# Results of a projection taken one group later beside attention, an output's remainder ahead of the next row maximum, and the products around them reordered, on one Trainium2 core

## The chip, the core and the metric

One core of a Trainium2 chip runs the whole program in one launch. Its engines run side by side, each through its own list of instructions, and wait for one another by semaphores: TensorE (PE; its weight loads are shown apart as PEld), VectorE (DVE), ScalarE (ACT), GpSimd (POOL), and SyncE (SP), which issues the weight transfers. The metric is the device time of one execution in microseconds (us).

## The reference

Two transformer networks follow each other, each of two layers, over 256 tokens of 1024 values; the first also carries 256 context tokens. First network: in each layer a gated feed-forward, a mixer (retention in layer 0, neighbourhood attention with 16 heads in layer 1), another feed-forward. Second network, cut to what matters here:

```
def second_block(x, positions, rel_bias, ...):
    for l in range(DEPTH):
        h = _rms_norm(x, norm_mix_pre[l])
        dq, dk, dv, mq, mk, mv, c_q, c_kv, k_pe, g = split(h @ w_in[l])
        oa = _diff_attention(dq, dk, dv, lam, rel_bias)      # 4 heads, two softmaxes each
        oa = _rms_norm(oa, diff_subln[l]) * (1.0 - lam_init)
        ob = _moba_attention(mq, mk, mv, rel_bias)           # 4 heads of 128
        q  = _rms_norm(c_q, mla_q_norm[l]) @ mla_w_uq[l]     # 8 heads, rope on 32 of 96
        kv = _rms_norm(c_kv, mla_kv_norm[l]) @ mla_w_ukv[l]
        oc = _dense_causal_attention(q, k, kv[v part], 1 / sqrt(96))
        br = stack(oa, ob, oc) @ w_branch[l]
        mixed = sum(sigmoid(g) * br) @ w_out[l]
        x = x + _rms_norm(mixed, norm_mix_post[l])
        h = _rms_norm(x, norm_mlp_pre[l])
        u = square(relu(h @ w_up[l]))
        x = x + _rms_norm(u @ w_down[l], norm_mlp_post[l])
    return x
```

Neighbourhood attention adds a bias per head and masks keys outside a window of 8 x 16 positions before the softmax. With 256 tokens MoBA has one block, so its attention is causal attention with a bias.

## The kernel before, in words

**One product.** Activations stay in SBUF, columns on partitions, tokens along a row. Every large product is float32 made of three fp32r products: high times high, high times low, low times high (`products`, matmul L1829). Weights come in blocks of 256 columns, 1024 deep, as two halves. SyncE loads them ahead into six raw slots; ScalarE copies a rounded high part (L808), VectorE subtracts it for the low part (L1215), each into one of three slots. A gemm is a list of groups, normally one block wide, two or four chunks of 128 columns or tokens each. TensorE writes the chunks in turn into four PSUM banks (gemm0 to gemm3); chunk n waits until chunk n − 4 is taken out. VectorE and ScalarE take it out as its kind says (`gemm` of each engine).

**The order** is written out by hand, once for each engine. `splits_upto` puts the splits of the next weight block between the chunks of the current one.

**Attention** is a generator of steps on each engine, a step for each head and half of 128 queries. TensorE issues scores (L1905; bias or mask L1906) into aux0 or aux1, turns the probabilities by a multiplication with a diagonal of inverse sums (L1922, aux2), and multiplies them with v (L1936, aux3). VectorE takes the row maximum (L1411, L1412), makes the diagonal (L1421, L1424; L1427 for the negated half of differential attention) and an output's low part (L1436); in neighbourhood attention it also adds the mask to a head's bias table (L1447). ScalarE makes exponentials (L974), copies turned probabilities out (L955) and the output's high part (L963).

**`alongside`** interleaves these steps with groups of other gemms: beside the four neighbourhood groups of four heads (`nat0` to `nat3`) the q, k, v of the next four heads, 9 groups in all; beside differential attention MoBA's k and v; beside latent attention (MLA) branch0, gate1, branch1 and gate2. `lag` says how many steps later than TensorE's list the other two engines' lists have the group: 1 beside the narrow attentions (differential, MoBA, MLA), 0 beside neighbourhood attention.

**The second network's layer** in order: the latents (mla_c), differential q, k, v, the two latent products (uq, ukv), MoBA's q with the rotations, differential attention, gate0, MoBA, MLA, branch2, the mixed product, then four pairs of up- and down-projection. Stages in the profiled execution: neighbourhood attention from 1817 to 2039 us, the second network from 2274; latent products from 2317, differential attention to 2417, MoBA to 2471, MLA to 2572, mixed product from 2607, feed-forward from 2656, and layer 1 from 2846.

## Time and profile before

| | |
|---|---|
| median of 3 runs | 3451.94 us (3451.68 to 3452.9) |
| the profiled execution | 3449.64 us |
| its span in the trace | 3447.9 us |
| TensorE busy | 3236.3 us, 94% |
| VectorE busy | 1879.9 us, 55% |
| ScalarE busy | 1151.5 us, 33% |
| chain that ended last | PE 86%, DVE 9%, ACT 3%, issue 2% |

Busy time is the union of an engine's instructions; matmuls are pipelined, and overlap by their modelled ends. PEclk is the TensorE clock that was granted, as a share of full speed. An arrow "<-" behind an instruction names what released it from a wait; "issue" means that nothing in the profile was waited for.

### The profile page before, as it was taken

What the parts mean: (1) busy time and instruction counts of PE and PEld (TensorE: products, weight loads), DVE (VectorE), ACT (ScalarE), POOL (GpSimd) and SP (SyncE); (2) the same over time, 40 slices, a digit from 0 to 9 for tenths busy, and PEclk for the clock granted to TensorE, in tenths of its full rate; (3) what the DMA queues carried; (4) which work ended last, traced back from release to release, by engine and by line L of the source; (5) the groups of instructions that cost most, each with busy time, mean ns of one, the idle gap of its engine ahead of it and who ended that gap; (6) DMA issues with size and microseconds to landing.
All of it is one profiled execution on the core that took longest, in us unless ns stands there. A gap on an engine that the chain in (4) does not pass through costs nothing.

```text
span 3447.9 us, 46967 instructions
## 1 busy us (share of the span) xinstructions
PE 3236.3 (94%) x19181; PEld 2794.8 (81%) x19181; DVE 1879.9 (55%) x3739; ACT 1151.5 (33%) x1945; POOL 38.5 (1%) x74
## 2 busy tenths in 40 slices
PE   8999999999899999999999999998898998888898
PEld 4788878888678888788877779996887998778798
DVE  1777663544468966433344345555456666445665
ACT  2322232323232222322233334442444344344442
POOL 1000000000000000000000000000000000000000
PEclk9999999999999999999989999998999999899899
DMA  8445441221145656323232125652234554224352
GB/s 254 122 146 170 129 141 62 92 68 62 61 123 169 216 171 189 86 80 110 80 100 66 61 81 153 178 176 74 86 103 150 163 167 125 62 86 147 110 183 87
DMA packets 501215, 421.36 MB, mean 122 GB/s; under 512 B 9947, under 2 KB 497675, under 8 KB 501001
## 3 DMA queue, kind: packets, MB, share of 16 engines
q1 hardware_dynamic: 497976, 412.33, 38.9%
q0 software_dynamic: 3024, 6.03, 0.7%
q8 instruction: 152, 2.49, 0.3%
q14 instruction: 63, 0.51, 0.0%
HBM read 417.20 MB, written 1.12 MB: 121 GB/s over the span
## 4 chain that ended last, share of the span: by engine, by line
PE 86%; DVE 9%; ACT 3%; issue 2%; SPq 0%; DMA 0%; DVEq 0%; ACTq 0%
PE gemm L1829 71%; DVE w_low L1215 3%; PE aux L1763 2%; PE aux L1922 2%; PE aux L1905 2%; PE aux L1936 2%; ACT w_high L808 1%; PE aux L1906 1%; PE gemm L1978 1%; PE aux L2067 1%; PE aux L1797 1%; DVE hf L1362 1%; DVE xt L1257 1%; DVE yt L1359 1%; PE aux L2055 1%
## 5 line engine op out<-in xcount | busy, mean ns | idle before, releaser
L1215 DVE TENSOR_TENSOR w_low<-raw,w_high 128x1024 fp32r<-128x1024 f32 (+2 forms) x720 | 759.1, 1096 | 369.8 <-ACT w_high L808 368.7
L808 ACT ACTIVATE w_high<-raw 128x1024 fp32r<-128x1024 f32 (+2 forms) x720 | 647.9, 948 | 692.4 <-PE gemm L1829 408.3
L1829 PE MATMUL gemm<-xh,w_high 128*128 128x512 f32 (+1 forms) x1792 | 676.9, 378 | 21.1 <-DVE xl L1243 21.1
L1829 PE MATMUL gemm<-xl,w_high 128*128 128x512 f32 (+1 forms) x1792 | 667.2, 372 | 0.0
L1829 PE MATMUL gemm<-xh,w_low 128*128 128x512 f32 (+1 forms) x1792 | 666.9, 372 | 0.0
L1829 PE MATMUL gemm<-yh,w_high 128*128 128x256 f32 x1344 | 392.2, 292 | 29.0 <-DVE yl L1386 10.2
L1829 PEld LDWEIGHTS gemm<-xh,w_high 128*128 128x128 f32 x1792 | 342.0, 191 | 93.2 <-issue 18.2
L1829 PEld LDWEIGHTS gemm<-xh,w_low 128*128 128x128 f32 x1792 | 342.2, 191 | 63.1
L1829 PEld LDWEIGHTS gemm<-xl,w_high 128*128 128x128 f32 x1792 | 342.7, 191 | 60.8 <-issue 0.7
L1829 PE MATMUL gemm<-yl,w_high 128*128 128x256 f32 x1344 | 384.5, 286 | 0.0
L1829 PE MATMUL gemm<-yh,w_low 128*128 128x256 f32 x1344 | 383.7, 286 | 0.0
L1186 DVE SCALAR_TENSOR_TENSOR macc<-raw,sc,macc 128x256 f32<-128x256 f32 x728 | 301.9, 479 | 4.0
L1829 PEld LDWEIGHTS gemm<-yh,w_high 128*128 128x128 f32 x1344 | 260.2, 194 | 37.2 <-issue 18.1
L1829 PE MATMUL gemm<-hid_high,w_high 128*128 128x512 f32 (+1 forms) x704 | 262.2, 372 | 0.0
L1829 PEld LDWEIGHTS gemm<-yl,w_high 128*128 128x128 f32 x1344 | 260.5, 194 | 0.1
L1829 PEld LDWEIGHTS gemm<-yh,w_low 128*128 128x128 f32 x1344 | 260.0, 193 | 0.0
L1829 PE MATMUL gemm<-hid_low,w_high 128*128 128x512 f32 (+1 forms) x704 | 259.5, 369 | 0.0
L1829 PE MATMUL gemm<-hid_high,w_low 128*128 128x512 f32 (+1 forms) x704 | 259.1, 368 | 0.0
L1829 PE MATMUL gemm<-act_high,w_high 128*128 128x256 f32 (+1 forms) x752 | 223.7, 298 | 30.9 <-DVE act_low L1365 17.9
L1829 PE MATMUL gemm<-act_low,w_high 128*128 128x256 f32 (+1 forms) x752 | 217.7, 290 | 0.0
L1829 PE MATMUL gemm<-act_high,w_low 128*128 128x256 f32 (+1 forms) x752 | 217.2, 289 | 0.0
L1349 DVE TENSOR_TENSOR hf<-sq,gemm 128x512 f32<-128x512 f32 (+1 forms) x88 | 54.5, 620 | 284.2 <-PE gemm L1829 284.2
(303 smaller groups left out, 4414.1 us busy)
## 6 DMA issues: line engine op xcount, KB each, us to landing
raw<-in_ffn_w_in SPq DMA_DIRECT2D x176, 512.0 KB, 5.3
raw<-in_w_mod SPq DMA_DIRECT2D x72, 1024.0 KB, 7.1
raw<-in_w_in SPq DMA_DIRECT2D x50, 1024.0 KB, 5.2
raw<-in_w_up SPq DMA_DIRECT2D x32, 1024.0 KB, 5.4
raw<-in_w_down SPq DMA_DIRECT2D x32, 1024.0 KB, 5.1
raw<-in_ffn_w_out SPq DMA_DIRECT2D x32, 768.0 KB, 4.6
raw<-in_ret_w_in SPq DMA_DIRECT2D x24, 1024.0 KB, 5.2
raw<-in_ffn_w_out SPq DMA_DIRECT2D x32, 640.0 KB, 4.1
```

The source lines that it names most:

```text
L808: act.activation(wh[i % SPL][:, a:b], raw[slot_of["w", i]][:, a:b], ACT.Copy).then_inc(w_high, 1)
L1186: dve.scalar_tensor_tensor(out=acc, in0=raw[slot][:, WB * k:WB * k + WB], scalar=sc[:, k, v:v + 1], in1=acc, op0=ALU.mult, op1=ALU.add).th ...
L1215: dve.tensor_tensor(wl[slot][:, a:b], raw[slot][:, a:b], wh[i % SPL][:, a:b].bitcast(F32), ALU.subtract).then_inc(w_low, 1)
L1257: dve.scalar_tensor_tensor(out=x_t[:, (N["s0"] + k) % 4, :], in0=N["src"](c)[:, ts * T:ts * T + T], scalar=N["scale"](c, ts), in1=mean_of( ...
L1349: dve.tensor_tensor(hf[:, pr % 2, 0:tok], sa[:, pr % 2, 0:tok], ps[:, 0:tok], ALU.mult).then_inc(odd_free, 1)
L1359: dve.scalar_tensor_tensor(out=yt[:, pr % 4, :], in0=ps[:, 0:T], scalar=0.0, in1=rb_of[name][0], op0=ALU.max, op1=ALU.mult).then_inc(free( ...
L1362: dve.tensor_tensor(hf2[:, pr % 2, :], yt[:, pr % 4, :], yt[:, pr % 4, :], ALU.mult).then_inc(hid_f, 1)
L1763: ins = pe.matmul(mean_of(N)[:, o:o + w], s_q[:, i % N["sqn"], P * j:P * j + P], fsq[:, c, :] if kind == "f" else ones[:, 0:1], start=c == ...
L1829: ins = pe.matmul(out, l_, r_, start=first and j == 0, stop=last and j == 2)
L1905: pe.matmul(sc_[:, 0:k], un["qk"][0], un["qk"][1], start=True, stop=True, skip_group_check=True)
L1922: ins = pe.matmul(aux[2][:, P * kt:P * kt + P], pe_[:, uq % a.slots, P * kt:P * kt + P], dg_[:, uq % a.slots, :], start=q == 0, stop=q == ...
L1936: ins = pe.matmul(aux[3][r0:r1, 0:P], tile["v"](kt), pt_[:, tg % 2, P * kt:P * kt + P], start=kt == 0, stop=kt == nkt - 1)
```

## The change

Seven edits; the matmuls are the same ones, but for four fewer small ones.

1. **Lag in groups.** `alongside` counts the lag in groups instead of steps, and neighbourhood attention gets a lag of 1 on VectorE and ScalarE.
2. **VectorE in attention.** The low part of output t − 2 stands before the next row maximum. A head's mask is one operation of 128 x 384 with a broadcast instead of six of 128 x 64.
3. **Latent products.** v of differential attention and of MoBA are gemms of one group each (`v_half`); the first half of differential v stands before uq, the second between uq and ukv. Groups of eight or more chunks (uq, ukv) split the next weights after chunk 5 instead of before chunk 0. The shared key's rotation is done after ukv, and its seven copies stand behind gate0.
4. **MoBA.** VectorE and ScalarE run the whole attention before they take out gate0's third group; TensorE's order stays.
5. **Gates and branches.** gate2 and branch2 are in quarters that alternate behind latent attention, which now has branch0, gate1, branch1 beside it. The mixed product reads ah/al and opens in the wide form (its first two groups together, k outermost, all four banks).
6. **Feed-forward of the second network.** The up-projection isn't scaled by the row of inverse roots; a ReLU on ScalarE and one product on VectorE give relu(x) · x, and ScalarE's high copy comes one chunk later. The missing scale enters the last norm's variance (`var_ready`).
7. **Start of the second network.** The last two squares are summed after row 3 of mla_c instead of row 7 (`joined`).

Its core as a diff ("..." where lines are left out):

```diff
@@ alongside, all engines
-                y = x - lag
-                upto = y * nb // na if not atts[name].narrow else 0 if y < 0 else 1 + y * (nb - 2) // na
-                while done < upto:
+                upto = 1 + x * (nb - 2) // na if atts[name].narrow else x * nb // na
+                while done < upto - lag:
...
@@ VectorE and ScalarE, neighbourhood groups
-                alongside(f"nat{g}", attention(f"nat{g}"), gemm, nxt)
+                alongside(f"nat{g}", attention(f"nat{g}"), gemm, nxt, 1)
...
@@ VectorE, attention
-                    for e in range(6):
-                        ins = dve.tensor_tensor(tt[:, hd % 2, e, :], tt[:, hd % 2, e, :], m, ALU.add)
-                    ins.then_inc(tt_masked, 1)
+                    dve.tensor_tensor(b, b, m.unsqueeze(1).to_broadcast([P, 6, 64]), ALU.add).then_inc(tt_masked, 1)
...
                     diagonal(j)
+                    if j and a.units[j - 1][0] != t and t >= 2:
+                        out_low(t - 2)
                     if j + a.lead < n:
                         row_max(j + a.lead)
-                    if j and a.units[j - 1][0] != t and t >= 2:
-                        out_low(t - 2)
...
@@ the list of gemms
+            def v_half(name, o, vb, q):
+                add(f"{name}_v{l}{q}", "token_scaled", B_groups(w, WB, 2, c00=o + 1024 + WB * q), Y, L,
+                    dst=lambda i, b=vb: b[:, i % 2, (i // 2) * WB:(i // 2 + 1) * WB], i0=2 * q)
...
+            for q in range(4):
+                gate(2, f"gate2{l}{q}", q, q + 1)
+                branch(2, f"branch2{l}{q}", q, q + 1)
...
         def with_mla(l):
-            return [f"{k}{l}" for k in ("branch0", "gate1", "branch1", "gate2")]
+            return [f"{k}{l}" for k in ("branch0", "gate1", "branch1")]
...
@@ VectorE and ScalarE, gemm
-                    splits_upto(s + 1)
+                    if len(ch) < 8:
+                        splits_upto(s + 1)
...
+                        if ci == 5 and len(ch) >= 8:
+                            splits_upto(s + 1)
...
@@ ScalarE, relu2
-                            act.wait_ge(hid_f, g.rl0 + i + 1)
-                            act.activation(ah[:, i, :], hf2[:, pr % 2, :], ACT.Copy).then_inc(hid_high, 1)
+                            act.wait_ge(chunk_ready, n + 1)
+                            if i >= 4:
+                                wait_chunk_out(act, n - 4)
+                            act.activation(yt[:, i % 4, :], ps[:, 0:T], ACT.Relu).then_inc(relu_ready, 1)
+                            for k in ([i - 1] if i else []) + ([i] if i == g.nch - 1 else []):
+                                wait_chunk_out(act, g.n0 + k)
+                                act.activation(ah[:, k, :], hf2[:, k % 2, :], ACT.Copy).then_inc(hid_high, 1)
...
@@ VectorE, relu2
-                            dve.scalar_tensor_tensor(out=yt[:, pr % 4, :], in0=ps[:, 0:T], scalar=0.0, in1=rb_of[name][0],
-                                                     op0=ALU.max, op1=ALU.mult).then_inc(free(n), 1)
-                            dve.wait_ge(free(n), n // 2 + 1)
-                            dve.tensor_tensor(hf2[:, pr % 2, :], yt[:, pr % 4, :], yt[:, pr % 4, :],
-                                              ALU.mult).then_inc(hid_f, 1)
...
+                            dve.wait_ge(relu_ready, g.rl0 + i + 1)
...
+                            dve.tensor_tensor(hf2[:, i % 2, :], yt[:, i % 4, :], ps[:, 0:T], ALU.mult).then_inc(free(n), 1)
...
@@ VectorE, inverses
+                if N["name"][:8] == "mlp_post":
+                    dve.wait_ge(sq_used, N["sq0"] + N["nc"])
+                    dve.scalar_tensor_tensor(out=joint[:, 2:4], in0=mean_of(N)[:, 0:2], scalar=1.0 / D, in1=joint[:, 0:2],
+                                             op0=ALU.mult, op1=ALU.add).then_inc(var_ready, 1)
...
@@ VectorE, rope and behind gate0
-                if k == MH:
-                    for hd in range(MH - 1):
-                        dve.tensor_copy(mk[R, hd, :], kpe[R, :]).then_inc(roped, 1)
...
+                for hd in range(MH - 1):
+                    dve.tensor_copy(mk[R, hd, :], kpe[R, :]).then_inc(roped, 1)
...
@@ VectorE and ScalarE, MoBA
-                steps = attention(f"moba{l}")
-                next(steps)
-                next(steps)
-                next(gate)
-                for x in range(len(atts[f"moba{l}"].units) - 1):
-                    next(steps)
-                run(steps)
+                run(attention(f"moba{l}"))
                 run(gate)
...
@@ TensorE, behind latent attention
-                pe.wait_ge(o_low, atts[f"mla{l}"].t1)
-                run(gemm(f"branch2{l}"))
-                run(gemm(f"mixed{l}", lambda kc: pe.wait_ge(mix_low, 8 * l + kc + 1)))
+                for q in range(4):
+                    run(gemm(f"gate2{l}{q}"))
+                    pe.wait_ge(o_low, atts[f"mla{l}"].t1)
+                    run(gemm(f"branch2{l}{q}"))
+                run(gemm(f"mixed{l}", lambda kc: pe.wait_ge(mix_low, 8 * l + kc + 1), wide=True))
...
@@ TensorE, joined
-                if k == DC - 1:
+                if k == 3:
                     for c in range(6, DC):
                         mean_square(norms["final"], c)
+                if k == DC - 1:
                     spread(norms["final"])
```

**Where instructions stand.** VectorE at the end of the first neighbourhood group (nat0) and the start of the next, before; `nv` is v of the next four heads, `nat_low` an output's low part, `stat` the maxima and sums:

```order
L1436 TENSOR_TENSOR nat_low<-aux3,nat_high 64x128 [waits attention_high_ready]
L1215 TENSOR_TENSOR w_low5<-raw5,w_high2 128x1024 [waits w_high_ready,odd_chunk_out,even_chunk_out]
L1215 TENSOR_TENSOR w_low5<-raw5,w_high2 128x1024 [waits w_high_ready]
L1332 TENSOR_SCALAR nv<-gemm1 128x256 [waits chunk_ready]
L1332 TENSOR_SCALAR nv<-gemm3 128x256 [waits chunk_ready]
L1436 TENSOR_TENSOR nat_low<-aux3,nat_high 64x128 [waits attention_high_ready] x2
L1411 TENSOR_REDUCE stat<-aux0 128x1 [waits probs_used,scores_ready]
```

And after the change (line numbers are those of the changed program):

```order
L1474 TENSOR_TENSOR nat_low<-aux3,nat_high 64x128 [waits attention_high_ready] x2
L1245 TENSOR_TENSOR w_low5<-raw5,w_high2 128x1024 [waits w_high_ready,odd_chunk_out,even_chunk_out]
L1245 TENSOR_TENSOR w_low5<-raw5,w_high2 128x1024 [waits w_high_ready]
L1372 TENSOR_SCALAR nv<-gemm1 128x256 [waits chunk_ready]
L1372 TENSOR_SCALAR nv<-gemm3 128x256 [waits chunk_ready]
L1449 TENSOR_REDUCE stat<-aux0 128x1 [waits probs_used,scores_ready]
L1450 TENSOR_SCALAR stat<-stat 128x1 [waits dve_chain]
```

Both low parts of the last outputs now stand ahead of the split and of the two copies of v, and the next group's first row maximum stands right behind the copies.

VectorE at the start of differential attention, before; `h` is MoBA's k, `dg2` the diagonals:

```order
L1421 RECIPROCAL stat2<-stat2 128x1 [waits probs_used,probs_ready]
L1424 TENSOR_SCALAR dg2<-cst,stat2 128x128 [waits dve_chain]
L1411 TENSOR_REDUCE stat2<-aux0 128x1 [waits probs_used,scores_ready]
L1412 TENSOR_SCALAR stat2<-stat2 128x1 [waits dve_chain]
L1215 TENSOR_TENSOR w_low0<-raw0,w_high0 128x1024 [waits w_high_ready,odd_chunk_out,even_chunk_out]
L1215 TENSOR_TENSOR w_low0<-raw0,w_high0 128x1024 [waits w_high_ready]
L1318 SCALAR_TENSOR_TENSOR h<-gemm2,rstd 128x256 [waits chunk_ready,r_row_ready]
L1318 SCALAR_TENSOR_TENSOR h<-gemm3,rstd 128x256 [waits chunk_ready]
L1421 RECIPROCAL stat2<-stat2 128x1 [waits probs_used,probs_ready]
L1427 TENSOR_SCALAR dg2<-cst,stat2,lam_negated 128x128 [waits dve_chain]
```

And after:

```order
L1459 RECIPROCAL stat2<-stat2 128x1 [waits probs_used,probs_ready]
L1462 TENSOR_SCALAR dg2<-cst,stat2 128x128 [waits dve_chain]
L1449 TENSOR_REDUCE stat2<-aux0 128x1 [waits probs_used,scores_ready]
L1450 TENSOR_SCALAR stat2<-stat2 128x1 [waits dve_chain]
L1459 RECIPROCAL stat2<-stat2 128x1 [waits probs_used,probs_ready]
L1465 TENSOR_SCALAR dg2<-cst,stat2,lam_negated 128x128 [waits dve_chain]
L1449 TENSOR_REDUCE stat2<-aux1 128x1 [waits probs_used,scores_ready]
L1450 TENSOR_SCALAR stat2<-stat2 128x1 [waits dve_chain]
```

The split and the two results of MoBA's first group are gone from between the maximum and the second diagonal; they stand further down.

VectorE in a group of the up-projection, before:

```order
L1215 TENSOR_TENSOR w_low3<-raw3,w_high0 128x1024 [waits w_high_ready] x2
L1359 SCALAR_TENSOR_TENSOR yt<-gemm0,rstd 128x256 [waits hidden_low_ready,chunk_ready]
L1362 TENSOR_TENSOR hf2<-yt 128x256 [waits even_chunk_out]
L1365 TENSOR_TENSOR act_low<-hf2,act_high 128x256 [waits hidden_high_ready]
L1359 SCALAR_TENSOR_TENSOR yt<-gemm1,rstd 128x256 [waits hidden_low_ready,chunk_ready]
L1362 TENSOR_TENSOR hf2<-yt 128x256 [waits odd_chunk_out]
L1365 TENSOR_TENSOR act_low<-hf2,act_high 128x256 [waits hidden_high_ready]
```

And after:

```order
L1245 TENSOR_TENSOR w_low3<-raw3,w_high0 128x1024 [waits w_high_ready] x2
L1398 TENSOR_TENSOR hf2<-yt,gemm0 128x256 [waits hidden_low_ready,relu_ready]
L1401 TENSOR_TENSOR act_low<-hf2,act_high 128x256 [waits hidden_high_ready]
L1398 TENSOR_TENSOR hf2<-yt,gemm1 128x256 [waits hidden_low_ready,relu_ready]
L1401 TENSOR_TENSOR act_low<-hf2,act_high 128x256 [waits hidden_high_ready]
```

A chunk has two operations instead of three, and the low part in a chunk's place is that of the chunk before it.

## Rows read from the trace of the kernel before

**Rows 1.** The page: busy time, share and instructions of each engine.
```profile
PE 3236.3 (94%) x19181; PEld 2794.8 (81%) x19181; DVE 1879.9 (55%) x3739; ACT 1151.5 (33%) x1945; POOL 38.5 (1%) x74
```

**Rows 2.** TensorE's waits, whole span: releaser: us in total, times, longest us.
```profile
PE aux L1936 <- issue: 24.4, 53, 0.9
...
PE aux L1922 <- DVE dg L1427: 21.0, 7, 4.6
PE gemm L1829 <- DVE act_low L1365: 17.9, 12, 4.0
PE aux L1922 <- DVE dg L1424: 13.7, 12, 3.2
PE aux L1922 <- ACT hf L955: 10.9, 6, 3.2
...
PE gemm L1829 <- DVE yl L1386: 10.2, 5, 4.0
...
PE gemm L1829 <- DVE mk L1332: 6.4, 2, 3.5
PE gemm L1829 <- DVE w_low L1215: 5.9, 2, 3.0
PE gemm L1829 <- ACT mq L914: 3.8, 1, 3.8
...
PE aux L2133 <- DVE mv L1332: 2.0, 2, 1.0
...
PE aux L1778 <- DVE r_columns L1232: 1.7, 1, 1.7
```

**Rows 3.** TensorE's waits, 1817 to 2039 us (neighbourhood attention).
```profile
PE aux L1936 <- issue: 10.1, 23, 0.9
PE aux L1922 <- DVE dg L1424: 2.5, 4, 0.6
```

**Rows 4.** Timeline around one output: start, us, engine, line, operation [idle before <-releaser].
```profile
1844.16 0.29 DVE L1436 TENSOR_TENSOR nat_low<-aux,nat_high 64x128 fp32r<-64x128 f32 x1
...
1844.49 0.91 DVE L1447 TENSOR_TENSOR tt<-tt,cst 128x64 f32<-128x64 f32 x6
...
1844.56 1.06 PE L1936 MATMUL aux<-hf,nv 128*64 128x128 f32 x8 [0.45 <-issue]
```

**Rows 5.** Timeline, end of the first neighbourhood group and start of the second.
```profile
1865.26 1.99 ACT L808 ACTIVATE w_high<-raw 128x1024 fp32r<-128x1024 f32 x2
...
1866.43 2.36 DVE L1215 TENSOR_TENSOR w_low<-raw,w_high 128x1024 fp32r<-128x1024 f32 x2 [0.76 <-ACT w_high L808]
...
1878.76 0.42 DVE L1332 TENSOR_SCALAR nv<-gemm 128x256 f32<-128x256 f32 x1 [5.17 <-PE gemm L1829]
...
1879.62 1.06 PE L1936 MATMUL aux<-hf,nv 128*64 128x128 f32 x8 [0.89 <-issue]
...
1880.60 1.12 PE L1905 MATMUL aux<-nk,nq 64*128 64x512 f32 x2
```

**Rows 6.** Timeline of TensorE, the second turn of differential attention, layer 0.
```profile
2372.84 1.22 PE L1922 MATMUL aux<-dg,pexp 128*128 128x128 f32 x4 [4.60 <-DVE dg L1427]
```

**Rows 7.** Stretches: us, busy PE, PEld, DVE, ACT, POOL, PEclk, DMA share, GB/s.
```profile
2372.00:2379.00 7.00, 6.16 (x23) 5.14 (x24) 3.32 (x16) 2.13 (x9) 0.00 (x0) 0.54 0.00 0
1868.00:1878.00 10.00, 10.00 (x88) 10.00 (x88) 1.22 (x2) 1.53 (x4) 0.00 (x0) 1.00 0.01 2
```

**Rows 8.** Timeline of ScalarE, two weight splits in branch2 of layer 0.
```profile
2594.02 1.99 ACT L808 ACTIVATE w_high<-raw 128x1024 fp32r<-128x1024 f32 x2
...
2600.38 1.99 ACT L808 ACTIVATE w_high<-raw 128x1024 fp32r<-128x1024 f32 x2
```

**Rows 9.** Timeline of VectorE, two weight splits in the first up-projection, layer 0.
```profile
2659.82 2.36 DVE L1215 TENSOR_TENSOR w_low<-raw,w_high 128x1024 fp32r<-128x1024 f32 x2 [0.53 <-ACT w_high L808]
...
2666.11 2.36 DVE L1215 TENSOR_TENSOR w_low<-raw,w_high 128x1024 fp32r<-128x1024 f32 x2 [0.53 <-ACT w_high L808]
```

**Rows 10.** The stretch of layer 1 of the second network, columns as in rows 7.
```profile
2846.00:3447.90 601.90, 528.88 (x3952) 499.65 (x3951) 344.34 (x699) 230.72 (x446) 0.00 (x0) 0.92 0.36 114
```

More of the change, by code:

```diff
@@ L1111, in _ @@
                 run(gemm(f"mla_c{l}"))
-                steps = both(*(gemm(f"diff_{k}{l}") for k in "qkv"))
+                steps = both(*(gemm(f"diff_{k}{l}") for k in "qk"))
                 next(steps)
@@ L1681, in _ @@
                 C = norms[f"c{l}"]
-                steps = both(*(gemm(f"diff_{k}{l}") for k in "qkv"))
+                steps = both(*(gemm(f"diff_{k}{l}") for k in "qk"))
                 next(steps)
+                if l == 0:
+                    rope_angles()
                 next(steps)
@@ L1855, in gemm @@
                     yield 1
-                for gi, (bl, ch) in enumerate(groups):
+                for gi, (bl, ch) in enumerate(groups, 2 * wide):
                     for bi, (_, k0, nk, w) in enumerate(bl):
@@ L1873, in gemm @@
                     if gi and name in follows:
-                        mean_square(follows[name], 2 * gi - 2)
-                        mean_square(follows[name], 2 * gi - 1)
+                        for c in range(0 if wide and gi == 2 else 2 * gi - 2, 2 * gi):
+                            mean_square(follows[name], c)
                     n += len(ch)
@@ L2114, in _ @@
                          after_row=opened("mix_pre1") if l else joined))
-                steps = both(*(gemm(f"diff_{k}{l}") for k in "qkv"))
+                steps = both(*(gemm(f"diff_{k}{l}") for k in "qk"))
                 next(steps)
```

165 lines of the change are left out of this document (97 added, 68 removed).

## The prediction

> **What bounds the kernel now.** I read four views. First the page's busy table and chain: TensorE is busy for 3236.3 of 3447.9 us, 94%, the others for 55% at most [rows 1]. The change leaves its work as it is (17,562 matmuls instead of 17,566), so time can only come from the 211.6 us in which it stands, and from its clock. Second, who TensorE waited for, over the whole span [rows 2]: the reader is to see that the largest entries are attention and the gemms that stand beside it. L1936 (probabilities times values) 24.4 us in 53 waits, L1922 (turning the probabilities) 21.0 + 13.7 + 10.9, the hidden products of the last feed-forward 17.9, the start of the mixed product 10.2 + 5.9, the latent projections 6.4 + 3.8 + 2.0. Third, the timeline around one wait of each kind. Fourth, the granted clock in stretches. Nothing before 1817 us changes.
>
> **Neighbourhood attention (1817 to 2039 us), gain.** Here VectorE takes an output's remainder (L1436) after the next row maximum (L1411), and the maximum waits for scores that TensorE has just issued. The remainder starts at 1844.16, directly behind the maximum, with no wait of its own, and TensorE's values start at 1844.56, after 0.45 us of standing [rows 4]; 23 such waits make 10.1 us [rows 3]. With the remainder first, it no longer waits for the maximum's scores; next in line are the turned probabilities, whose turn TensorE issued before. I take all 10.1 us (bounds 6 to 13, the upper one because matmuls then overlap). The mask as one operation instead of six is VectorE time beside TensorE's and counts nothing; if that cover failed the six cost 0.91 us a head [rows 4], so the edit is worth less than that.
>
> **Neighbourhood attention, loss.** The lag goes from none to one whole group. Three groups (q, k, v of the next four heads) are issued during eight steps, so v is issued at the last step and its results are now taken after the end of the attention. TensorE opens the next attention by waiting for exactly these results. Before, v was taken while TensorE still multiplied, and values and next scores stood 0.98 us apart (1879.62, 1880.60) [rows 5]. Now the order on VectorE is: two remainders, a weight split, two copies of v; the second remainder needs the values that TensorE issues after v. From the rows: the values last 1.06 and the high part about as long as the remainder, 0.29; VectorE's split starts 1.17 us after ScalarE's and lasts 2.36; two copies at 0.42 [rows 4, 5]. 1.06 + 0.29 + 1.17 + 2.36 + 0.84 = 5.7 us instead of 0.98, so 4.7 us, at three transitions 14 us. Queued behind the copies on VectorE is the first row maximum, so nothing else fills the hole. To this comes the clock. After a stall of 4.60 us before the turn at 2372.84 [rows 6], the stretch 2372 to 2379 shows a granted clock of 0.54, that is near the 1.2 GHz level, with TensorE busy for 6.16 of 7 us [rows 7]; half of that, 3.1 us, is work that the full 2.4 GHz would have saved. Three times 3.1 is 9 us. The stage as a whole: 10 − 14 − 9 = 13 us slower (bounds 4 faster, 20 slower).
>
> By the Trainium skill, "TensorE: Matmul & The Clock Gate", section "Terms", the penalty of throttled time is about that time times the share of pulses that the gate withholds, so half of it here. The stretch above agrees as far as TensorE is bound there; by the rule alone, three stretches of 7 us would cost 10.5 us instead of the 9 that I take.
>
> **Latent projections and rotation, gain.** Half of the v product now stands between the two latent products, the split of the next weights comes after chunk 5 rather than ahead of all the chunks, and the 7 copies of the rotated key leave this place. The waits for mk (6.4), mq (3.8) and mv (2.0) sum to 12.2 us for both layers [rows 2]. A new one arises: the key's rotation now comes after the last chunk, and TensorE's fourth rotation waits for it; three operations at 0.42 and the late split cost about 2 us a layer. 12 − 4 = 8 us (bounds 3 and 12).
>
> **Differential attention, gain.** Before, VectorE takes the first group one step after TensorE issued it, when TensorE has no other group to do: the next diagonal stands behind a split and two copies, 4.60 us at 2372.84 [rows 6]. After, it takes a group in the step in which TensorE issues the next one; at the full clock 88 matmuls of 128 x 256 run in 10 us [rows 7], so a group's 48 take 5.5. Of the 21.0 us in 7 waits, four of about the longest's 4.6 (18 together) go, 3 stay [rows 2]. Each dragged down the clock; four times 3.1 is 12 us, of which I take half, since the small matmuls there may hold it down by themselves: 6. Bounds 12 and 32 for the two, taken 24.
>
> **MoBA and latent attention, gain.** L1936 outside of the neighbourhood stage is 24.4 − 10.1 = 14.3 us, L1922 behind L1424 13.7 less 2.5 at the starts of neighbourhood groups, 11.2, and L1922 behind L955, 10.9 [rows 2, 3]: 36.4 us. Both causes above apply, and MoBA no longer has a gate group between its first steps. But four gate groups leave the cover of latent attention in each layer, and about five steps there now run without a product. I take three quarters, 27 us (bounds 12 and 36).
>
> **Gates, branches, mixed product: a small loss.** Before, TensorE waits 10.2 + 5.9 = 16.1 us at the start of the mixed product [rows 2]. A branch group takes ScalarE and VectorE 6.36 us from split to split when the split is of 1024 columns [rows 8], TensorE 24 matmuls, 2.7. A gate group is 5.5 on TensorE; on the others my estimate is half a branch group, 3.2. A pair so costs them 9.6 against 8.2, so over four pairs they fall behind by 4 × 1.4 = 5.6 us, and the wide start of the mixed product needs all four banks, the last branch's two among them, whose five operations of 0.42 each come to 4.2. That makes 9.8 us of standing a layer, 19.6 for both instead of 16.1: 3.5 us slower (bounds 12 slower, 10 faster).
>
> **Last feed-forward, gain.** A group of up-projection takes the two engines 6.29 us (2659.82 to 2666.11) [rows 9], more than TensorE's 5.5, so they fall behind and TensorE waits at each down-projection: 17.9 us [rows 2]. Now VectorE has two operations a chunk instead of three and ScalarE's copy is one chunk late, so the cycle is about 2.36 + 4 × 0.42 plus its wait of 0.53 [rows 9], under 5 us. And the row of inverse roots is gone from the opening. I count 0.9 for the extra variance step: 17 us, and 3 for the clock after the wait of 4.0 us, the longest. Taken 20 (bounds 12 and 25). ScalarE's new operation is covered by its idle half.
>
> **Opening of the second network.** The last two squares are summed after row 3 instead of row 7, so the inverse root is ready: 1.7 us [rows 2].
>
> **Sum.** −13 + 8 + 24 + 27 − 3.5 + 20 + 1.7 = 64.2 us faster. The profiled execution took 3449.64 us (span 3447.9, 1.7 around it), 2.3 under the median of the runs. 3449.6 − 64.2 = 3385, my forecast.
>
> **Rivals.** (a) *The gain halves.* The attention terms (24 + 27) bring a third, because the next late one in each step is ScalarE's exponential, which no part of the change makes earlier; against it, the remainder is plainly the last one in [rows 4]. 3385 + 34 = 3419. (b) *It ends slower: banks are freed too late.* A result taken one group later holds its bank one group longer, and there are four. 9 + 8 + 24 = 41 groups stand beside attention. From 64/41 = 1.6 us of bank wait each the gain is eaten; with a split and a copy (2.36 + 0.42 = 2.8) each it is 115 us, and the kernel takes 3385 + 115 = 3500. For it: v in the neighbourhood stage has four chunks, all banks at once. Against: TensorE's next group in order is issued after VectorE's step of the same number, and the split that it needs comes two groups ahead. (c) *Nothing comes of it:* every wait is replaced, as in the neighbourhood stage; 3450. The four long waits with a free engine behind them speak against it. (d) *The clock comes back whole.* From 2846 us the mean granted clock is 0.92 [rows 10]: 2 × 0.08 × 601.9 = 96 us at the low level in one layer. If the idle pieces that precede it go, half, 48 us, returns, in the first layer about as much; beyond the 9 counted that may be 45 us: 3340. The skill's rule on the clock (same page, section "HAM oscillation — how this bites in real kernels") says that such stretches repeat with each wait, which bears on this; against it, stretches at the low level fall in attention that no long wait precedes.
>
> **How the numbers follow.** Forecast 0.64 (3362 to 3410), (a) 0.20, (d) 0.07, (b) 0.06, (c) 0.03. The range that should hold 8 in 10 leaves out (b), (c), (d) and the upper end of (a): 3360 to 3426. This kernel's runs tell 0.2%, 7 us, from no change. Faster: 0.91; within: 0.03; slower: 0.06.
>
> **What the profile after would show.** L1936's "issue" waits almost gone; three new waits of 4 to 5 us at the first scores of the neighbourhood groups 2 to 4, each followed by a low clock; no wait over 2 us before a turn in differential, MoBA and latent attention; one wait of 5 to 8 us at the start of each mixed product; down-projections with under 0.5 us. The forecast is wrong if waits for freed banks show up before gemm groups beside attention, or if L1922 keeps its total.

## The result and the profile after

The changed kernel takes 3343.9 us (median of 4 runs, 3342.3 to 3345.5), the kernel before 3451.8 in the same comparison: ratio 0.969, 95% interval 0.9673 to 0.9707. Forecast were 3385 us with a range from 3360 to 3426. The gain is 108 us where 64 were forecast; the time lies below the range, next to rival (d), which had 3340 us and a chance of 0.07.

The page after; it answers to [rows 1].

```profile
PE 3201.1 (96%) x19173; PEld 2765.6 (83%) x19173; DVE 1844.6 (55%) x3599; ACT 1164.8 (35%) x2007; POOL 38.5 (1%) x74
```

The page counts 19,173 matmuls instead of 19,181 (the 17,562 and 17,566 of the prediction stand in no view), and TensorE is busy for 35 us less. With practically the same work that is for the most part a faster clock; the other 69 of the 104 us of span are standing. The waits of TensorE after, over the whole span (us in total, times, longest us), answer to [rows 2]:

```profile
PE gemm L1864 <- DVE yt L1411: 17.2, 4, 7.3
PE aux L1940 <- issue: 14.3, 3, 4.8
...
PE aux L1957 <- ACT hf L988: 7.1, 12, 1.1
...
PE aux L2172 <- DVE mk L1704: 4.5, 2, 2.3
PE aux L1957 <- DVE dg L1465: 4.0, 8, 1.4
...
PE aux L1957 <- DVE dg L1462: 3.7, 6, 1.0
```

The reader is to see what is gone: the 53 "issue" waits before the values (24.4 us), the long ones before a turn (21.0, 13.7 and 10.9 are 4.0, 3.7 and 7.1), and those of the down-projections (17.9). What is new are two lines with long single waits: three of 4.8 us at the first scores (L1940) of neighbourhood groups 2 to 4, and two of about 7.3 us for banks at the start of the mixed products (in the first line). The stall at a neighbourhood group stands in the timeline of the changed kernel:

```profile
1877.57 1.09 PE L1971 MATMUL aux<-hf,nv 128*64 128x128 f32 x8
1878.70 0.27 ACT L996 ACTIVATE nat_high<-aux 64x128 fp32r<-64x128 f32 x1 [11.44 <-PE aux L1971]
1879.00 0.30 DVE L1474 TENSOR_TENSOR nat_low<-aux,nat_high 64x128 fp32r<-64x128 f32 x1 [10.53 <-ACT nat_high L996]
1880.18 2.36 DVE L1245 TENSOR_TENSOR w_low<-raw,w_high 128x1024 fp32r<-128x1024 f32 x2 [0.88 <-ACT w_high L830]
1882.57 0.76 DVE L1372 TENSOR_SCALAR nv<-gemm 128x256 f32<-128x256 f32 x2
1883.43 2.04 PE L1940 MATMUL aux<-nk,nq 64*128 64x512 f32 x2 [4.77 <-issue]
```

The chain is the one that the prediction counted. The two scores behind the stall take 2.04 us where the same pair takes 1.12 in [rows 5]: they run at the low level.

**By stages.** The same pieces of work in both kernels, columns as in [rows 7]. Before: neighbourhood attention; all behind it; differential attention of layer 0 and of layer 1; of layer 0 MoBA, latent attention with its gates and branches, the mixed product, the feed-forward.

```profile
1818.99:2039.14 220.15, 204.15 (x1217) 156.78 (x1217) 87.45 (x279) 70.75 (x159) 18.14 (x28) 1.00 0.21 61
2039.14:3447.90 1408.76, 1266.13 (x9696) 1208.95 (x9696) 806.10 (x1553) 566.04 (x1050) 4.79 (x9) 0.94 0.42 129
2358.32:2417.86 59.54, 48.80 (x281) 39.61 (x281) 22.18 (x75) 15.72 (x51) 0.00 (x0) 0.86 0.17 54
2940.04:3004.60 64.56, 54.17 (x281) 43.82 (x281) 22.35 (x75) 16.05 (x51) 0.00 (x0) 0.76 0.16 49
2438.47:2471.24 32.77, 25.61 (x178) 23.30 (x177) 15.85 (x56) 13.29 (x44) 0.00 (x0) 0.95 0.15 47
2471.24:2594.95 123.71, 110.90 (x832) 103.65 (x832) 68.78 (x168) 49.88 (x122) 0.00 (x0) 0.96 0.42 132
2594.95:2632.99 38.04, 29.12 (x225) 28.28 (x224) 22.11 (x32) 16.70 (x26) 0.00 (x0) 0.91 0.42 132
2656.28:2845.15 188.87, 178.95 (x1472) 176.80 (x1472) 122.25 (x189) 76.03 (x103) 0.00 (x0) 0.98 0.53 168
```

After, in the same order:

```profile
1818.85:2056.62 237.77, 220.22 (x1216) 166.26 (x1216) 83.31 (x205) 70.18 (x159) 18.14 (x28) 0.91 0.19 57
2056.62:3343.70 1287.08, 1217.57 (x9688) 1172.35 (x9688) 775.23 (x1493) 579.86 (x1112) 4.79 (x9) 0.97 0.45 141
2361.08:2406.37 45.29, 43.30 (x281) 34.98 (x281) 21.95 (x75) 15.18 (x51) 0.00 (x0) 1.00 0.24 70
2890.11:2935.40 45.29, 43.30 (x281) 34.98 (x281) 21.90 (x75) 15.17 (x51) 0.00 (x0) 1.00 0.23 71
2426.98:2454.79 27.81, 24.22 (x178) 22.06 (x177) 16.12 (x56) 12.79 (x44) 0.00 (x0) 1.00 0.18 55
2454.79:2566.26 111.47, 106.27 (x832) 99.84 (x832) 72.55 (x174) 50.84 (x123) 0.00 (x0) 1.00 0.47 146
2566.26:2602.39 36.13, 28.83 (x225) 28.77 (x224) 17.99 (x27) 15.55 (x24) 0.00 (x0) 0.86 0.42 137
2624.38:2798.99 174.61, 174.49 (x1472) 174.16 (x1472) 107.53 (x159) 84.15 (x133) 0.00 (x0) 1.00 0.57 183
```

The granted clock is the column behind POOL. Neighbourhood attention is 17.6 us longer, and its clock fell from 1.00 to 0.91. Everything behind it is 121.7 us shorter: TensorE stands for 69.5 us instead of 142.6 (us less PE busy), 73 less, and is busy for 49 less at a clock of 0.97 instead of 0.94. Differential attention, MoBA, latent attention and feed-forward all run at 1.00 now.

### The profile page after: what moved, and what is told of

It is laid out like the page before. It is cut to its first block and busy times, and to the rows that moved or that the text cites. A ratio compares the mean times of both kernels' runs of the same rounds, so it can differ in the third digit from the quotient of the medians.

```text
span 3343.7 us, 46943 instructions
## 1 busy us (share of the span) xinstructions
PE 3201.1 (96%) x19173; PEld 2765.6 (83%) x19173; DVE 1844.6 (55%) x3599; ACT 1164.8 (35%) x2007; POOL 38.5 (1%) x74
## 3 DMA queue, kind: packets, MB, share of 16 engines
HBM read 417.20 MB, written 1.12 MB: 125 GB/s over the span
## 5 line engine op out<-in xcount | busy, mean ns | idle before, releaser
L1864 PE MATMUL gemm<-xh,w_high 128*128 128x512 f32 (+1 forms) x1792 | 675.4, 377 | 22.8 <-DVE xl L1281 22.8
L1864 PE MATMUL gemm<-xl,w_high 128*128 128x512 f32 (+1 forms) x1792 | 665.9, 372 | 0.0
L1864 PE MATMUL gemm<-xh,w_low 128*128 128x512 f32 (+1 forms) x1792 | 665.6, 371 | 0.0
L1864 PEld LDWEIGHTS gemm<-xh,w_high 128*128 128x128 f32 x1792 | 341.1, 190 | 94.4 <-issue 18.4
L1864 PEld LDWEIGHTS gemm<-xh,w_low 128*128 128x128 f32 x1792 | 341.1, 190 | 63.0
L1864 PEld LDWEIGHTS gemm<-xl,w_high 128*128 128x128 f32 x1792 | 341.6, 191 | 60.6 <-issue 0.7
L1864 PE MATMUL gemm<-yh,w_high 128*128 128x256 f32 x1216 | 351.7, 289 | 16.9 <-DVE yl L1306 7.1
L1864 PE MATMUL gemm<-yl,w_high 128*128 128x256 f32 x1216 | 345.9, 284 | 0.0
L1864 PE MATMUL gemm<-yh,w_low 128*128 128x256 f32 x1216 | 345.4, 284 | 0.0
L1864 PE MATMUL gemm<-act_high,w_high 128*128 128x256 f32 (+1 forms) x880 | 252.4, 287 | 14.5 <-DVE yt L1411 14.5
L1864 PE MATMUL gemm<-hid_high,w_high 128*128 128x512 f32 (+1 forms) x704 | 262.1, 372 | 0.0
L1864 PE MATMUL gemm<-hid_low,w_high 128*128 128x512 f32 (+1 forms) x704 | 259.5, 369 | 0.0
L1864 PE MATMUL gemm<-hid_high,w_low 128*128 128x512 f32 (+1 forms) x704 | 259.2, 368 | 0.0
L1864 PEld LDWEIGHTS gemm<-yh,w_high 128*128 128x128 f32 x1216 | 233.4, 192 | 22.6 <-issue 17.3
L1864 PE MATMUL gemm<-act_low,w_high 128*128 128x256 f32 (+1 forms) x880 | 249.4, 283 | 0.0
L1864 PE MATMUL gemm<-act_high,w_low 128*128 128x256 f32 (+1 forms) x880 | 249.3, 283 | 0.0
L1864 PEld LDWEIGHTS gemm<-yl,w_high 128*128 128x128 f32 x1216 | 233.5, 192 | 0.1
L1864 PEld LDWEIGHTS gemm<-yh,w_low 128*128 128x128 f32 x1216 | 233.1, 192 | 0.0
```

Source lines behind the costliest of these rows:

```text
L1864: ins = pe.matmul(out, l_, r_, start=first and j == 0, stop=last and j == 2)
```

## The experiments

Theory: a long wait of TensorE costs itself and then a stretch at the 1.2 GHz level; the gain beyond the forecast is clock that came back with the waits. Rival: the low stretches belong to attention's small matmuls and not to the waits. Times are medians; ratios are to the kernel before, measured on the same chip.

### No lag in neighbourhood attention

```diff
-                alongside(f"nat{g}", attention(f"nat{g}"), gemm, nxt, 1)
+                alongside(f"nat{g}", attention(f"nat{g}"), gemm, nxt)
```

> The changed kernel with the lag of neighbourhood attention on VectorE and ScalarE back at none; all else stays. Clock theory (each wait of 4.77 us costs itself and then 10 to 14 us at the 1.2 GHz level): the stage goes from 237.8 us to about 210 (14.3 us of waits, 16 us of clock, less 2 of other standing), the kernel from 3344 to about 3316, and the stage shows no low clock. Rival (only the waits count, the clock falls through the small matmuls of attention themselves): 3344 - 14 = 3330 and low stretches stay.

Measured: 3319.2 us, ratio 0.9614 (0.960 to 0.9629). The stage:

```profile
1818.22:2030.40 212.18, 203.24 (x1216) 156.78 (x1216) 83.19 (x205) 70.02 (x159) 18.14 (x28) 1.00 0.22 63
```

212.2 us instead of 237.8, at full clock. The lag alone so costs 25.6 us. What is left of the change in this stage, the order of the low part and the mask in one operation, gains 220.15 − 212.18 = 8.0 (taken 10.1 for the order alone). How the 25.6 us divide is less clear: the three long waits are 14.3 us, which leaves 11 for the clock; but by the rows TensorE is busy for 17.0 us less (220.22 to 203.24) and stands for 8.6 less, because without the lag other, short waits come up in place of the long ones.

### The wait filled with matmuls

```diff
+                if name in ("nat1", "nat2", "nat3"):
+                    for r in range(20):
+                        pe.matmul(aux[1][:, 0:512], xh[:, r % DC, 0:P], xh[:, r % DC, 0:T2],
+                                  start=True, stop=True, skip_group_check=True)
                 wait_gemm_out(pe, after)
```

> The changed kernel with 20 matmuls of 128x512 that nobody reads put before each of the three waits at the start of neighbourhood groups 2 to 4 (about 4.6 us, as long as the wait). The dependencies stay as late as they were. Clock theory: the 41 us at the low level in this stage vanish, the stage goes from 237.8 to about 221, the kernel to about 3328, though not one wait got shorter. Rival (the waits themselves and the lag cost it): no gain, 3344 or a little more.

Measured: 3332.7 us, ratio 0.9653 (0.9637 to 0.9669). The stage, with 60 matmuls more:

```profile
1818.59:2043.30 224.71, 219.03 (x1276) 168.81 (x1276) 83.02 (x205) 69.46 (x159) 18.16 (x28) 0.99 0.21 60
```

No result came earlier, and the stage is 13.1 us shorter. That is the price of the clock behind three waits of 4.77 us by itself, about 4.4 each. The 14.3 us that TensorE was kept waiting are still there, only busy.

### The same in the kernel before, in differential attention

```diff
+                    if name[:4] == "diff" and j in (1, 9):
+                        if a.t0 + t >= 1:
+                            pe.wait_ge(pt_out, a.t0 + t)
+                        for r in range(19):
+                            pe.matmul(aux[2][:, 0:512], yh[:, r % DC, 0:P], yh[:, 0:2, :],
+                                      start=True, stop=True, skip_group_check=True)
                     pe.wait_ge(dg_ready, u + 1)
```

> The kernel before with 19 matmuls of 128x512 that nobody reads put ahead of the turn in each of the four places where TensorE waits 4.5 to 4.6 us for a diagonal of differential attention. No dependency comes earlier. Clock theory: the low stretches of the two differential attentions (17 and 31 us) mostly vanish, these stages go from 59.5 and 64.6 us to about 51 each, the kernel to about 3452 - 20 = 3432. Rival (the small matmuls themselves hold the clock low there, which is why I counted half): under 6 us.

Measured: 3433.0 us, ratio 0.9937 (0.9915 to 0.9958). The two differential attentions:

```profile
2359.41:2414.30 54.89, 52.28 (x319) 42.11 (x319) 21.98 (x75) 15.37 (x51) 0.00 (x0) 1.00 0.19 58
2934.18:2989.00 54.82, 52.20 (x318) 42.03 (x318) 22.06 (x75) 15.38 (x51) 0.00 (x0) 1.00 0.19 58
```

They go from 59.5 and 64.6 us to 54.9, with the small matmuls as they were and a granted clock of 1.00 instead of 0.86 and 0.76. So the rival falls: the waits brought the clock down. 4.7 + 9.7 = 14.4 us of this stage's gain are clock; the other 2 × 9.6 us (54.9 to 45.3) are the four waits, for the most part. The whole kernel is 21 us faster by the medians and 16 by the spans of the two profiled executions (3447.9, 3431.8); the stages account for 14.4. The prediction's argument against rival (d), that low stretches fall in attention where no long wait stands before them, does not hold here either: with four waits filled the clock is 1.00 in the whole of both stages.

### The low part behind the maximum again

```diff
-                    if j and a.units[j - 1][0] != t and t >= 2:
-                        out_low(t - 2)
                     if j + a.lead < n:
                         row_max(j + a.lead)
+                    if j and a.units[j - 1][0] != t and t >= 2:
+                        out_low(t - 2)
```

> The changed kernel with the output's low part behind the next row maximum again, in all four attentions. If the low part is the last one that TensorE's values wait for: the 24.4 us of short waits come back, 10 of them in neighbourhood attention, 3344 + 24 = 3368 or a little less. Rival (a), the next late one is ScalarE's exponential: under 8 us, 3352 at most.

Measured: 3359.4 us, ratio 0.9732 (0.9718 to 0.9747), 15.4 more than the changed kernel. The short waits are back as they were:

```profile
PE aux L1971 <- issue: 24.8, 52, 0.7
```

But 24.8 us of waits cost 15. Other waits become shorter in their place (L988 is 2.2 us here, 7.1 in the changed kernel), so a part of the 24 us would have been waited for something else. That is a piece of rival (a), a third of the term and not two thirds. In neighbourhood attention the order alone is worth 5.7 us (243.5 instead of 237.8 us), with the lag in place.

### Lag counted in steps again, narrow attentions

```diff
-                upto = 1 + x * (nb - 2) // na if atts[name].narrow else x * nb // na
-                while done < upto - lag:
+                y = x - lag
+                if atts[name].narrow:
+                    upto = 0 if y < 0 else 1 + y * (nb - 2) // na
+                else:
+                    upto = x * nb // na - lag
+                while done < upto:
```

> The changed kernel with the lag of the narrow attentions (differential, latent) counted in steps again; neighbourhood attention as changed. Clock theory: the four long waits of differential attention come back (18 us) with about 48 us at the low level behind them (24 us), and some of latent attention: about 3344 + 42 = 3386. Rival (only standing counts): 3344 + 17 = 3361.

Measured: 3438.8 us, ratio 0.9959 (0.9944 to 0.9974): 95 us slower than the changed kernel, over twice what either theory gave. Differential attention accounts for 14.6 + 17.4 (59.9 and 62.7 us), about as expected. The miss is latent attention, layer 0 and layer 1:

```profile
2466.72:2609.00 142.28, 117.73 (x832) 109.88 (x832) 72.49 (x174) 51.42 (x123) 0.00 (x0) 0.89 0.37 114
3043.34:3185.50 142.16, 117.94 (x832) 110.07 (x832) 72.52 (x174) 51.42 (x123) 0.00 (x0) 0.89 0.37 115
```

142.3 us each, against 111.5 after and 123.7 before. TensorE's waits in the first of these stretches:

```profile
PE aux L1961 <- DVE dg L1466: 15.4, 5, 4.7
PE aux L1961 <- ACT hf L992: 6.7, 2, 4.1
```

What follows is read from the order in the program and was not run by itself. Before, 16 groups stood beside 16 steps, so in nearly every step TensorE had a group while VectorE took the last one. With gate2 moved out 12 are left, and at a lag of one step VectorE takes a group in a step in which TensorE may have none. Moving gate2 out while counting in steps so seems to cost about 19 us a layer (142.3 against 123.7); counting in groups repairs that and more (111.5). The two edits have to be read together. The prediction gave them one term and did not price the first without the second.

### Gate0's third group within MoBA again

```diff
-                run(attention(f"moba{l}"))
+                steps = attention(f"moba{l}")
+                next(steps)
+                next(steps)
+                next(gate)
+                for x in range(len(atts[f"moba{l}"].units) - 1):
+                    next(steps)
+                run(steps)
                 run(gate)
```

> The changed kernel with gate0's third group taken out by VectorE and ScalarE after two steps of MoBA attention, as before. If that group was what the second turn waited for (3.2 us, with low clock behind it): two waits of 3.2 us and 3.4 us at the low level each return, 3344 + 10 = 3354, the stage from 27.8 us to about 33. Rival (the order of the low part had done it): within 3 us of 3344.

Measured: 3356.5 us, ratio 0.973 (0.9715 to 0.9744), 12.6 more. The wait of 3.2 us is back in each layer, with its clock (0.95 from 2427 to 2460 us, where MoBA of the changed kernel has 1.00): TensorE's waits in MoBA of layer 0 begin with

```profile
PE aux L1969 <- ACT hf L988: 4.7, 3, 3.2
```

### The hidden values' copy in its own chunk

```diff
-                            for k in ([i - 1] if i else []) + ([i] if i == g.nch - 1 else []):
+                            for k in [i]:
```
(in both places, ScalarE and VectorE)

> The changed kernel with ScalarE's high copy and VectorE's low part of the hidden values in the chunk's own place instead of one chunk later. If the gain of the feed-forward comes from two operations in place of three on VectorE alone: no change, 3344 within 3. If the later copy is needed, the cycle of a group is 2 x (0.42 + hand-over to ScalarE and back) longer, about 6.3 us as before, and the waits before the down-projections come back: 3344 + 20 to 28.

Measured: 3357.0 us, ratio 0.9714 (0.9693 to 0.9734), 13 more. Between the two: of the feed-forward's 28 us gain, 13 need the late copy; 15 are left for the two operations and the missing row, which no run separates. The stage takes 181.5 us in layer 0 instead of 174.6. It has one wait of 3.2 us before the first down-projection, where it was 4.0 before, and beside this line only what the changed kernel has too:

```profile
PE gemm L1864 <- DVE act_low L1401: 3.4, 2, 3.2
```

### Waits of eight lengths among dense products

```diff
                                 dve.wait_ge(hid_high, g.hid0 + k + 1)
+                                if k == g.nch - 1 and i == k:
+                                    for _ in range(DOSES[name]):
+                                        chain(dve.tensor_tensor(al[:, k, :], hf2[:, k % 2, :],
+                                                                ah[:, k, :].bitcast(F32), ALU.subtract))
```

> The changed kernel; in each of the eight up-projections VectorE repeats the low part of the last chunk 6, 9, 11, 13 (layer 0), 16, 20, 26 and 32 times (layer 1), which delays the down-projection by a wait that grows from about 0 to 11 us, in the middle of products that keep TensorE busy. Clock theory: short waits of a microsecond or two leave the clock at the 2.4 GHz level, those of about 4 us and more are each followed by 7 to 14 us at the 1.2 GHz level, whatever the matmuls are. Rival (only attention's small matmuls bring the clock down): granted clock 1.00 in all eight.

One profile. The waits came out as 2.7, 3.5, 4.4 and 5.3 us in layer 0, 7.3, 8.6, 11.3 and 14.1 in layer 1. The shortest and the longest:

```profile
2641.03 0.58 PE L1870 MATMUL gemm<-act_high,w_high 128*128 128x256 f32 x1 [2.71 <-DVE act_low L1407]
...
3379.26 0.58 PE L1870 MATMUL gemm<-act_high,w_high 128*128 128x256 f32 x1 [14.08 <-DVE act_low L1407]
```

And the 10 us behind the waits of 2.7, 4.4, 8.6, 11.3 and 14.1 (behind the other three it is 61 to 66 matmuls):

```profile
2641.03:2651.03 10.00, 10.00 (x62) 10.00 (x63) 5.92 (x9) 2.01 (x2) 0.00 (x0) 0.70 0.26 80
2745.40:2755.40 10.00, 10.00 (x71) 10.00 (x72) 5.66 (x7) 2.01 (x2) 0.00 (x0) 0.83 0.35 107
3258.36:3268.36 10.00, 10.00 (x73) 10.00 (x74) 5.66 (x7) 2.01 (x2) 0.00 (x0) 0.85 0.34 107
3316.75:3326.75 10.00, 10.00 (x61) 10.00 (x62) 5.65 (x7) 2.01 (x2) 0.00 (x0) 0.69 0.27 81
3379.26:3389.26 10.00, 10.00 (x65) 10.00 (x66) 5.65 (x7) 2.62 (x4) 0.00 (x0) 0.75 0.00 0
```

At full clock 88 matmuls fit into 10 us [rows 7]; here it is 61 to 73. So each wait cost 1.7 to 3.1 us of work beyond itself ((88 − n) × 0.114), and that doesn't grow with the wait. In the following 10 us it is 86 or 87 again, at a clock of 1.00. One reason why it doesn't grow can be read off the waits themselves, the one of 4.4 us and the one of 14.1:

```profile
2741.00:2745.40 4.40, 0.00 (x0) 0.00 (x0) 4.09 (x11) 0.73 (x1) 0.00 (x0) 1.00 0.49 174
3365.20:3379.26 14.06, 0.01 (x1) 0.01 (x1) 13.03 (x32) 0.81 (x1) 0.00 (x0) 0.57 0.00 1
```

Behind the shorter one the clock is low only for work; in the longer one it is low for about 12 us (2 × 0.43 × 14.06) in which TensorE has nothing to do, and that costs nothing. The expectation put the full effect at about 4 us and more; 2.7 us are enough. In the changed kernel's neighbourhood attention the low level lasted longer. The 15 us behind its three stalls:

```profile
1883.43:1898.43 15.00, 15.00 (x39) 8.10 (x39) 4.63 (x14) 3.80 (x9) 1.29 (x2) 0.57 0.05 13
1952.36:1967.36 15.00, 15.00 (x52) 8.74 (x53) 5.86 (x17) 3.92 (x10) 2.30 (x4) 0.71 0.07 15
2019.39:2034.39 15.00, 15.00 (x38) 8.28 (x38) 4.64 (x14) 3.80 (x9) 1.29 (x2) 0.55 0.05 13
```

A clock of 0.57, 0.71 and 0.55 over 15 us is 12.9, 8.7 and 13.5 us at the low level, against 3 to 6 in the products. Behind waits of about the same length the low level so stays longer in attention, though TensorE is busy for all of the 15 us there. What in attention does it, no run here separates.

### The mixed product begun in stages

On the kernel without the lag in neighbourhood attention:

```diff
+                        for gi, (bl, ch) in enumerate(pair):
+                            pe.wait_ge(w_low, 2 * (s + gi) + 2)
+                            for ci in range(2):
+                                wait_chunk_out(pe, n + 2 * gi + ci - 4)
+                                for k in range(6):
+                                    if k not in seen:
+                                        x_waits(k)
+                                        seen.add(k)
+                                    products(n + 2 * gi, s + gi, 0, bl, ch, ci, k)
...
-                    for k in range(DC):
+                    for k in range(6, DC):
```

> The changed kernel without the lag in neighbourhood attention (3319 us), and with the mixed product begun in stages: six of the eight k for its first two chunks, whose banks and weights are there early, then for the third and the fourth, each behind its own bank, then the last two k for all four. If the wide start waits for the last branch's banks (7.3 us, with 10.2 us at the low level behind it), most of it goes: 3319 - 2 x (6 + 4) = 3299. Rival (the chain through the last branch on VectorE and ScalarE sets the time anyway): 3316 or more.

Measured: 3306.1 us, ratio 0.9566 (0.9543 to 0.959), 13 less than without the stages. The start waits 0.7 us for weights instead of 7.3 us for banks:

```profile
2541.14 0.36 PE L1864 MATMUL gemm<-act_high,w_high 128*128 128x256 f32 x1 [0.70 <-DVE w_low L1245]
```

The whole mixed product, layer 0, which took 36.13 us at a clock of 0.86:

```profile
2540.43:2568.88 28.45, 26.89 (x225) 26.48 (x224) 17.85 (x27) 15.57 (x24) 0.00 (x0) 1.00 0.55 176
```

7.7 us less in a layer. TensorE stands for 1.6 us instead of 7.3, since waits of 0.6 and 0.2 us come up beside the one of 0.7; that is 5.7 of it. It is busy for 1.9 less (28.83 to 26.89), which is the clock, where 4 were expected. Of the 15.4 for both, 13 reach the end.

### All of it, and the norms' waits filled

The staged kernel, with matmuls that nobody reads ahead of the first product behind the norms:

```diff
+            FILL = {'in000': 11, 'ret_q0': 11, 'ret_out3': 44, 'in010': 11, 'in100': 11, 'nat_q0': 11, 'in110': 8,
+                    'up00': 10, 'up10': 10, 'mla_c1': 10}
...
+                    for r in range(FILL.get(name, 0)):
+                        pe.matmul(bank[m % 4][:, 0:512], wh[s % SPL][:, 0:P], wh[s % SPL][:, 0:512],
+                                  start=True, stop=True)
```

> The kernel with no lag in neighbourhood attention and the staged mixed product (3306 us), and with matmuls of 128x512 that nobody reads ahead of the first product behind ten norms and the last output of retention, 8 to 11 each (2 to 2.5 us, as long as TensorE waits there) and 44 at retention's (10 us). They write the bank that the product overwrites, and no dependency comes earlier. Clock theory: of the low stretches outside of attention (7 to 17 us each in ten places) most vanish: 3306 - 30 = 3276. Rival (at these places the small matmuls of the norm, and not the wait, bring the clock down, or the filling delays the product): 3306 or above.

Measured: 3298.8 us, ratio 0.956 (0.9544 to 0.9576), the fastest of all; whether it beats the staged one by 7 us or by 2 (by the two ratios) is inside their intervals. The clock did come back: over the whole span it is 0.985 instead of 0.977, some 53 us less at the low level (2 × (0.023 × 3304.9 − 0.015 × 3297.8)). The expected 30 us did not. The first 12 us of retention's first product, filled and then unfilled:

```profile
504.06:516.06 12.00, 8.73 (x32) 5.15 (x31) 10.78 (x28) 8.91 (x17) 0.00 (x0) 1.00 0.01 1
```

```profile
502.68:514.68 12.00, 10.80 (x29) 6.30 (x30) 11.19 (x29) 8.64 (x16) 0.00 (x0) 0.74 0.00 1
```

The clock is back (1.00 instead of 0.74), and TensorE still issues about as many matmuls, 32 and 29, busy for less of the time. VectorE is busy for 10.8 and 11.2 of the 12 us, mostly with the split activations that each step of the product needs. The first steps, three matmuls each, follow one another at 1.57 us in both kernels (505.12, 506.70, 508.27 filled; 504.16, 505.74, 507.31 unfilled): at the low level TensorE's work just fits into VectorE's step, at the full one TensorE waits 0.61 us in each. The low clock cost nothing there, because another engine set the pace. The fill was also too long. The first matmul of the product unfilled, and the fill with the first matmul behind it:

```profile
502.68 0.77 PE L1864 MATMUL gemm<-xh,w_high 128*128 128x512 f32 x1 [2.63 <-DVE xl L1281]
```

```profile
500.66 3.56 PE L1874 MATMUL gemm<-w_high 128*128 128x512 f32 x11
504.06 0.40 PE L1866 MATMUL gemm<-xh,w_high 128*128 128x512 f32 x1
```

The product starts 1.4 us later for it, as the rival said. How the other nine places divide between the two reasons stays open.

## Why the prediction was wrong

The direction, the places and nearly all mechanisms held; the sum was too small by 40 us, and the failed term is the clock.

- **The step that failed:** in differential attention it said "four times 3.1 is 12 us, of which I take half, since the small matmuls there may hold it down by themselves: 6", in the feed-forward 3, and none elsewhere. Shown by filling the waits of the kernel before: with the same small matmuls the clock is 1.00, and the two stages are 14.4 us shorter. Over everything behind neighbourhood attention the clock went from 0.94 of 1408.8 us to 0.97 of 1287.1, so 2 × 0.06 × 1408.8 = 169 us at the low level became 77; half of the difference is 46 us, where 9 were counted. The clock is read to hundredths, which leaves some 14 us either way on that half; TensorE's busy time over the same stretch, 1266.1 to 1217.6, gives 49. The standing behind neighbourhood attention was nearly right: 73 us went, and the terms other than clock add up to 68. So rival (d) had the mechanism. That its number, 3340, is so near is luck: "48 us in a layer, in the first about as much" less the 9 counted is 87 and not 45, and gives 3298. The clock came back by about half and not whole; layer 1 had 96 us at the low level before (0.92 of 602.75 us) and has 44 after (0.96 of 544.7).
- **Neighbourhood attention**, −13: measured −17.6. Gain 8.0 (taken 10), waits 14.3 (taken 14: 4.77 each against 4.7), clock 11 as the rest without the lag (17 by TensorE's busy time) and 13 by the filled kernel (taken 9). The row of 7 us from which 3.1 a stall was taken is shorter than these stretches, with 8.7 to 13.5 us at the low level.
- **Latent products, opening,** 8 + 1.7: measured 14.7 us from the end of neighbourhood attention to differential attention in layer 0, about 4 in layer 1, 18.5 where 9.7 were taken. In layer 0 8.5 of it are standing and 6.2 TensorE's busy time (304.54 to 298.30), so clock again, which this term did not have. The wait of 2.3 us at a rotation came as forecast (4.5 for both). No run took these edits back.
- **Differential attention,** 24: measured 14.3 + 19.3 = 33.5; waits 19 (taken 18), clock 14 (taken 6).
- **MoBA, latent attention, gates, mixed product,** 27 − 3.5: measured 5.0 + 12.2 + 1.9 in layer 0 and as much in layer 1, 38. The expected fall-behind over the gate and branch pairs did happen: waits of 1.4 and 1.1 us and then 7.3, 9.8 in all as forecast (5.6 + 4.2, though five operations of 0.42 make 2.1 and only twice that is 4.2). But latent attention lost all its long waits and its low clock, which outweighs it.
- **Feed-forward,** 20: measured 14.3 a layer, 28.5. The waits are gone (0.1 us of standing in 174.6 us) and with them the low clock; the late copy is worth 13 of it.
- **Rivals.** (a) holds for a third of the low part's term (24.8 us of waits cost 15). (b) did not happen: the four waits for a bank in the changed kernel (L1864 behind yt, 17.2 us) stand at the mixed products and at the first gate quarters, none at a group beside attention. (c) held for neighbourhood attention alone.

By the Trainium skill, "TensorE: Matmul & The Clock Gate", section "HAM oscillation — how this bites in real kernels", a stall that recurs brings the throttled level back each time and costs half of the throttled time. The two kernels agree behind neighbourhood attention: about 92 us less at the low level, 49 us less TensorE busy time. The filled kernel does not: some 53 us less at the low level gave 7 us, and at retention's first product, where VectorE sets the pace, none. The prediction named the section and gave its rival 0.07.

## What to carry to other kernels

Price a wait of the engine that bounds the kernel as the wait plus the low clock behind it, here 2.7 to 14 us of waiting plus 1.7 to 3.1 us among dense products and about 4 in attention, and read the second part from the granted clock over the whole stretch until it is back, not from a few us. Filling the wait with matmuls that nobody reads separates the two. It paid by itself in neighbourhood and differential attention; before retention's first product, where VectorE sets the pace, it gave nothing, and a fill longer than the wait delays the product. When results are to be taken later, look at the last group before a consumer: a lag that saved 95 us inside the narrow attentions (against this kernel with the lag in steps) lost 26 where the next stage opens with the delayed results.

## What the runs showed of the hardware

Eight waits of 2.7 to 14.1 us before dense products, in one profile, were all followed by a stretch at the 1.2 GHz level, and its price in work was 1.7 to 3.1 us without growing with the wait. After three waits of 4.77 us before neighbourhood attention's matmuls the level stayed low for 9 to 14 us. Useless matmuls of the wait's length kept the clock at 0.99 to 1.00. The changed kernel's differential attention of layer 0, whose longest wait is 1.4 us, has 1.00 from end to end.
